# A two-layer hybrid decoder on eight cores: norm steps bound to engines, a later queueing rule in its planner, six residual tiles kept in SBUF, first loads in another order

## The reference

```
h = h + 1/2 * gate1 * SwiGLU_1(mod1(RMSNorm(h)))
h = h + gate2 * W_out[ SGU_heads(P) || DilatedAttn_heads(P) ],  P = mod2(RMSNorm(h)) @ W_in
h = h + 1/2 * gate3 * SwiGLU_2(mod3(RMSNorm(h)))
```

## Time and profile before

| | |
|---|---|
| three timed runs | 5645.67, 5723.91, 5064.55 us (median 5645.67) |
| profiled execution | 5035.81 us |
| its span, slowest core (2) | 5034.3 us; all cores 4988.7 to 5034.3 |
| PE / DVE / ACT / POOL busy | 95% / 54% / 39% / 23% of the span |
| DMA | 866.37 MB, mean 172 GB/s |

### The profile page before, as it was taken

How to read it: one execution, slowest core, us unless ns; L and a number is a source line. 1 busy time by engine, 2 the same in 40 slices (tenths; PEclk the granted TensorE clock), 3 DMA queues, 4 the chain that set the end, 5 groups by cost and what they waited for, 6 DMA issues and landing times.

```text
span 5034.3 us, 75361 instructions; the slowest of 8 cores (4988.7 to 5034.3 us)
## 1 busy us (share of the span) xinstructions
PE 4797.4 (95%) x25784; PEld 2274.2 (45%) x26282; DVE 2739.8 (54%) x4359; ACT 1957.7 (39%) x2862; POOL 1147.0 (23%) x955
## 2 busy tenths in 40 slices
PE   4999989989999999999999999999999999999998
PEld 1444434444445544444444444444444455544443
DVE  7542676483775464773433327755638654536424
ACT  4111556353554443411311126644536553524211
POOL 4001561131550101400200016402136200023101
PEclk9999999999999999999999999999999999999999
DMA  8968674687565686882621385757575545474237
GB/s 237 216 123 220 184 193 122 182 239 202 163 188 164 176 227 174 262 239 66 211 95 38 92 241 156 194 140 203 138 206 175 171 127 158 113 239 156 96 98 258
DMA packets 389049, 866.37 MB, mean 172 GB/s; under 512 B 151456, under 2 KB 184608, under 8 KB 382240
## 3 DMA queue, kind: packets, MB, share of 16 engines
q1 hardware_dynamic: 371344, 773.02, 49.6%
q0 software_dynamic: 17328, 88.49, 11.2%
HBM read 766.36 MB, written 241.17 MB: 200 GB/s over the span
## 4 chain that ended last, share of the span: by engine, by line
PE 77%; DMA 7%; DVE 5%; issue 4%; ACT 3%; POOL 2%; SPq 1%; DVEq 0%; POOLq 0%; ACTq 0%
PE ps L925 42%; PE ps L953 21%; PE ps L1052 6%; PE ps L1355 3%; PE ps L1293 3%; PE ps L1270 2%; DMA hS<-arena 2%; DMA arena<-hS 1%; DMA arena<-ada_w 1%; DVE arena L1112 1%; POOL arena L1121 1%; DVE arena L879 1%; DMA arena<-wdS 1%; DVE arena L860 1%; DMA vS<-arena 1%
## 5 line engine op out<-in xcount | busy, mean ns | idle before, releaser
L925 PE MATMUL ps<-arena 128*128 128x512 bf16 x10957 | 2486.5, 381 | 54.6 <-ACT arena L884 16.8
L925 PEld LDWEIGHTS ps<-arena 128*128 128x128 bf16 x11264 | 1077.4, 98 | 1308.4 <-issue 59.2
L953 PE MATMUL ps<-arena 128*128 128x512 bf16 x5501 | 1228.0, 380 | 19.8 <-DMA arena<-wdS 10.2
L931 ACT ACTIVATE arena<-ps 128x512 f32<-128x512 f32 x704 | 419.2, 597 | 1327.7 <-PE ps L925 1312.2
L953 PEld LDWEIGHTS ps<-arena 128*128 128x128 bf16 x5632 | 547.3, 98 | 673.2 <-issue 23.8
L933 DVE SCALAR_TENSOR_TENSOR arena<-arena,ps 128x512 f32<-128x512 f32 x704 | 480.4, 684 | 623.1 <-ACT arena L931 621.7
L957 DVE SCALAR_TENSOR_TENSOR arena<-ps,arena 128x512 f32<-128x512 f32 x256 | 192.0, 750 | 833.5 <-PE ps L953 794.0
L853 ACT ACTIVATE arena<-arena 128x512 f32<-128x512 f32 x448 | 270.0, 625 | 865.2 <-DMA arena<-hS 537.5
L1052 PE MATMUL ps<-arena 128*128 128x512 bf16 x2528 | 575.7, 386 | 21.8 <-DVE arena L1112 6.2
L938 DVE TENSOR_TENSOR arena<-ps,arena 128x512 bf16<-128x512 f32 x704 | 484.7, 690 | 185.0 <-PE ps L925 161.0
L860 POOL TENSOR_TENSOR arena<-arena 128x512 f32<-128x512 f32 (+1 forms) x236 | 316.0, 1339 | 1066.2 <-ACT arena L853 987.7
(11 more groups left out here) (71 smaller groups left out, 2600.2 us busy)
## 6 DMA issues: line engine op xcount, KB each, us to landing
arena<-wguS SPq DMA_DIRECT2D x242, 512.0 KB, 5.9
arena<-hS SPq DMA_DIRECT2D x192, 512.0 KB, 7.2
arena<-wdS SPq DMA_DIRECT2D x136, 704.0 KB, 7.2
arena<-ada_w SPq DMA_DIRECT2D x144, 512.0 KB, 6.2
hS<-arena SPq DMA_DIRECT2D x248, 256.0 KB, 5.8
arena<-hS SPq DMA_DIRECT2D x184, 256.0 KB, 6.0
wguS<-wgu POOLq DMA_DIRECT2D x66, 512.0 KB, 7.6
hS<-arena SPq DMA_DIRECT2D x64, 512.0 KB, 6.7
```

Source lines behind the costliest of these rows:

```text
L925: main([(lambda e, kc=kc, half=half, bk=bk, y=y, gu=gu: e.matmul(bank(bk), lhsT=gu[:, half, kc, :], rhs=y[:, kc, :], start=(kc == 0), stop ...
L931: G.op([act(lambda e, sg=sg, gb=gb: e.activation(out=smv[sg.i], in_=bank(gb), func=AF.Tanh, scale=0.5), 490, "tanh")], reads=[gb], writes= ...
L953: main([(lambda e, j=j: e.matmul(bank(bk), lhsT=wd[:, j, :], rhs=a[:, j, :], start=(j == 0), stop=(j == FC - 1)), [bwd, ba[j]], MM) for j ...
```

## The change

1. **The planner.** A side task that feeds others no longer gets a latest time of at most 30 us after its place; only what it feeds counts. A task that is no DMA, whose margined landing lies ahead and whose L is over 5 us past PE's next matmul, is not queued until the margined landing.
2. **Fixed engines.** sqsum and ropeadd, oamul, anorm go to POOL alone, nu to DVE alone, ny to ACT alone, vnorm to ACT or POOL. Only the norms of the first four tiles and of the last two keep a choice.
3. **Tiles summed in place.** `downs` takes tiles that are loaded whole at its start: tile 0, and tiles 4 and 6, of the first SwiGLU in both layers (whose next norm starts from SBUF and no longer loads them), and tiles 4 to 7 of the last SwiGLU, whose sums are not stored any more. Tile 7 was in place before, so six are new in that sense. Tiles 6 and 7 of the end share their down weights, tile 7 one chunk behind.
4. **First loads.** c and tile 0 of the input come first, then the rows of `ada_w`; the constants and the other tiles come later; the first weights get due times.

```
 priorities
-            L = t.cur + 30000.0
+            L = 1e12 if t.succ else t.cur + 30000.0
 schedule, pick
+                if not t.dma and t.mready > now and t.L > hp + 5000.0:
+                    nxt = min(nxt, t.mready)
+                    continue
 norm_sum(ht, pos, alts=False)
-                G.op([pool(f, 1250), dvex(f, 615)], reads=[ba, bq], writes=[bo], name="sqsum", pos=pos)
+                G.op([dvex(f, 615), pool(f, 1280)][:1 + alts] if alts else [pool(f, 1280)], reads=[ba, bq], writes=[bo], name="sqsum", pos=pos)
 norm_y
-                G.op([dvex(f, 615), pool(f, 1300)], reads=[brs], writes=[bh], name="nu", pos=pos)
+                G.op([dvex(f, 615), pool(f, 1700)][:1 + alts], reads=[brs], writes=[bh], name="nu", pos=pos)
-                      dvex(g, 420), pool(g, 1500)],
+                      dvex(g, 420)][:1 + alts],
 proj
-                            out=o, in_=i_, func=AF.Identity, scale=sc, bias=bi), 390), pool(f, 500), dvex(f, 200)],
+                            out=o, in_=i_, func=AF.Identity, scale=sc, bias=bi), 390), pool(f, 500)],
-                        G.op([pool(f, 1300), dvex(f, 650)], reads=[a0[1], a1[1]], writes=[bo], name="ropeadd")
+                        G.op([pool(f, 1400)], reads=[a0[1], a1[1]], writes=[bo], name="ropeadd")
-                    G.op([pool(f, 1300), dvex(f, 615)], reads=[bzt, ugs[hd][1]], accw=[boa], name="oamul", pos=pos)
+                    G.op([pool(f, 1300)], reads=[bzt, ugs[hd][1]], accw=[boa], name="oamul", pos=pos)
 normalise
-                        G.op([pool(f, 1300), dvex(f, 615)], reads=[ba, br], accw=[bo], name="anorm", pos=pos, part=h)
+                        G.op([pool(f, 1300)], reads=[ba, br], accw=[bo], name="anorm", pos=pos, part=h)
 FFN.downs
-            def downs(self, tiles, dst=None):
-                for m in range(KC):
-                    wd, bwd = load_wd(self.l, self.w, m, G.M)
-                    for t in tiles:
-                        self.down(t, m, wd, bwd, dst)
+            def downs(self, tiles, dst={}, keep=True, lag=0):
+                wd = {}
+                for t in dst:
+                    load_h(dst[t], t, self.src, self.bsrc, G.M)
+                for m in range(KC + lag):
+                    if m < KC:
+                        wd[m] = load_wd(self.l, self.w, m, G.M)
+                    for n, t in enumerate(tiles):
+                        k = m - lag * n
+                        if 0 <= k < KC:
+                            self.down(t, k, wd[k][0], wd[k][1], dst.get(t), keep)
 first loads
-            G.dma("sp", lambda e: e.dma_start(out=cb, in_=src), 524288, writes=[bcb], name="cb", pos=p0)
+            G.dma("sp", lambda e: e.dma_start(out=cb, in_=src), 524288, writes=[bcb], name="cb", pos=p0,
+                  due=None if due is None else due - 90000.0)
+                      due={1: -16000.0, 2: -13000.0, 3: -8000.0}.get(j))
-        cond(range(16), -3000.0, steps(WD0 + 4096, 4096, 3) + steps(ACT[0], 4096, 5), WD0, -26000.0)
+        cond(range(16), -3000.0, steps(WD0 + 4096, 4096, 3) + steps(ACT[0], 4096, 5), WD0, -28000.0)
 the stages
-            f1.downs((0, 1))
+            h0 = HT(HB)
+            f1.downs((0, 1), {0: h0})
+            norm_y(h0, 0, l, 1, pm)
+            nrm(1, 1, pm + 15000.0, H)
-            fa.downs((4, 5))
+            h4 = HT(HB)
+            fa.downs((4, 5), {4: h4})
-            fa.downs((6, 7))
+            h6 = HT(HB)
+            fa.downs((6, 7), {6: h6})
-                fc.downs((4, 5))
+                hts = {4: HT(HB), 5: HT(GU0)}
+                fc.downs((4, 5), hts, False)
-                fc.downs((6,))
-                fc.downs((7,), ht)
-                norm_out(norm_load(6, hS, bHS, G.M, GU0), 6, G.M - 25000.0)
-                norm_out(ht, 7, G.M, True)
+                hts = {6: HT(ACT[0]), 7: HT(ACT[1])}
+                fc.downs((6, 7), hts, False, 1)
+                norm_out(hts[6], 6, G.M, True)
+                norm_out(hts[7], 7, G.M, True)
```

More of the change, by code:

```diff
@@ L783, in load_gu @@
             if (l, w) == (0, 0) and (l, w, j) not in kept:
-                G.dma("pool", lambda e: e.dma_start(out=ap, in_=wgu_d[l, w, j]), 1048576, writes=[b], name="guf", pos=pos)
+                G.dma("pool", lambda e: e.dma_start(out=ap, in_=wgu_d[l, w, j]), 1048576, writes=[b], name="guf", pos=pos,
+                      due={1: -16000.0, 2: -13000.0, 3: -8000.0}.get(j))
                 G.dma("sp", lambda e: e.dma_start(out=wguS[l, w, j], in_=ap), 524288, reads=[b], writes=[bWG[l, w, j]],
@@ L869, in norm_sum, with norm_y @@
             return rs, brs
-        def norm_y(ht, slot, l, i, pos):
-            rs, brs = norm_sum(ht, pos)
+        def norm_y(ht, slot, l, i, pos, alts=False):
+            rs, brs = norm_sum(ht, pos, alts)
             y, by = tile(Y0 + 8192 * slot, [128, KC, T], BF16, KC, "y")
@@ L939, in gates, with down @@
                                   610)], reads=[ub, sg], writes=[ba[j]], name="hid", pos=p)
-            def down(self, t, m, wd, bwd, dst=None):
+            def down(self, t, m, wd, bwd, dst=None, keep=True):
                 a, ba = self.act[t]
@@ L1366, in outproj, with norm_load @@
             return ht
-        def norm_load(t, src, bsrc, pos, off=HB):
+        def norm_load(t, src, bsrc, pos, off=HB, due=None):
             ht = HT(off)
-            load_h(ht, t, src, bsrc, pos)
+            load_h(ht, t, src, bsrc, pos, due)
             return ht
         for ap, src, n in ((ng_sb, ngv, "ng"), (adab, ada_b, "adab"), (fg_sb, fgv, "fg"), (lngb, lngb_d, "lngb")):
-            G.dma("sp", lambda e, ap=ap, src=src: e.dma_start(out=ap, in_=src), 65536, writes=[bC[n]], name="const", pos=-20000.0, due=-90000.0)
+            G.dma("sp", lambda e, ap=ap, src=src: e.dma_start(out=ap, in_=src), 65536, writes=[bC[n]], name="const", pos=-20000.0, due=-21000.0)
         memset(ones_bf, 1.0, bC["ones"])
@@ L1388, in nrm @@
                 s, b = (src, bsrc) if src_ is None else src_
-                norm_y(norm_load(t, s, b, pos, off), t % 4, l, i, pos)
+                first = l == 0 and i == 0 and t == 0
+                norm_y(norm_load(t, s, b, pos, off, -60000.0 if first else None), t % 4, l, i, pos, l == 0 and i == 0 and t < 4)
             H = (hS, bHS)
@@ L1411, in build_nc @@
                 mx0.load(c, ACT[0] + 8192 * n, True, p2)
-            nrm(0, 1, pm, H)
-            nrm(1, 1, pm + 30000.0, H)
             mx0.open()
@@ L1434, in build_nc @@
             q3 = G.M
-            nrm(4, 1, q2, H)
+            norm_y(h4, 0, l, 1, q2)
             nrm(5, 1, q2 + 40000.0, H)
@@ L1451, in build_nc @@
                 if t == 4:
-                    nrm(6, 1, p4, H)
+                    norm_y(h6, 2, l, 1, p4)
                 if t == 5:
```

14 lines of the change are left out of this document (6 added, 8 removed).

## The result

Timed side by side, the changed kernel took 5546.82, 5004.09, 5733.06 and 5752.98 us (median 5639.94), the kernel before 5645.67, 5723.91, 5064.55 and 5073.81 us (median 5359.74). What is left gives a ratio of 0.9869 (0.9826 to 0.9911), 1.3% less. The profiled execution went from 5035.81 to 5004.09 us: 31.7 us less, where 59 less was forecast.

What follows compares the result with a forecast made beforehand. PE was taken to bound the kernel, busy 4797.4 of 5034.3 us, through its idle time and lower clock. Terms 30 + 12 + 8 + 9 + 0 = 59 us off 5035.81 gave 4977 us, range 4910 to 5040.

Steps and rivals of the forecast that it cites:

- more than that: Projections: many small PE waits also come from DVE's queue; 116 us less in all, 4920 us; chance 0.20.
- the waits move: Whole kernel: every removed wait is replaced, only the end and the tile in place gain; 5019 us; chance 0.17.
- VectorE's case: Projections: eight nu in a row on DVE delay rope if each takes over 1.76 us; 5107 us; chance 0.07.
- POOL's cases: Projections of tiles 0 to 3: POOL's added work outlasts PE's, cancelling the 30 us gain; 5041 us; chance 0.06.
- the 0.52 of clock to an idle microsecond: Four projection stretches: 40.6 us lost to lower clock over 78.6 us idle, so removed waits count 1.52 times.
- Fixed engines, 30 us: Projections: PE's waits for DVE's vnorm and last statistics go, 19.7 us, with clock 30; bounds nothing to 79.
- The later rule, 12 us: Side operations held until loads land: a good half of PE's 21.6 us exp and mask waits; bounds 0 to 27.
- Tiles in place, 8 us: Tile 0 goes to its next norm without store and loads: 5.3 us of ny waits, with clock 8; bounds 0, 8.
- The end, 9 us: Last tiles: down-weight waits 10.2 us and about 4 of clock go, later products cost 5.4; bounds 4 and 14.
- The start, 0: First gate 8.5 us earlier, but three norms follow it instead of two; bounds 9 us gained or lost.
- What should have shown it wrong: Projections: nu over 1.76 us with PE awaiting rope, POOL over 90%; new sqsum or nsum waits; first gate after 60 us.
- the signs of being right: No DVE vnorm or ropeadd waits, projection idle about 59 us, no late down-weight waits, earlier gate, shorter ACT square waits.

Runs made afterwards that it cites:

- e3: The kernel before with only the later queueing rule added: 5031 us, 5 less than the kernel before, ratio 0.9979.
- e10: The changed kernel without its queueing rule, on chip 0: 4978 us, 54 less than the kernel before, ratio 0.9902.
- e9: The whole changed kernel run again with more executions, on chip 0: 4945 us, 88 less than the kernel before, ratio 0.9831.
- e5: The whole changed kernel run again, unchanged, on chip 3: 4958 us on 3 of 8 dies, 80 less than the kernel before.

## Why the prediction was right or wrong

**The number.** The step that failed is that the sum starts from the profiled execution and takes the execution to be timed for one of that kind: a die that is held at a lower granted clock is put at nothing and lies outside the range, although two of the three timed runs on the table were 5645.67 and 5723.91 us. In three of the four executions timed, one die ran at a mean clock of 0.83 to 0.87, which makes the median 5639.94 us where 4977 was forecast. Executions of the profiled kind took 5001 to 5004 us at first, and 4945 and 4958 on dies at 0.98 or more later. Why a die is held at a lower clock in one execution and not in another, no run here shows.

**The size of the change.** 59 us were forecast, 32 measured at first, 80 to 88 without the 0.81. That lies between two of the cases, the forecast (4950 to 5005) and *more than that* (4920), so the forecast is too small, in the two terms named below; *the waits move*, VectorE's and POOL's cases are out.

**The reading behind it.** The 236.9 and 78.6 us of idle time came from a core with 498 matmuls unrecorded; the cores with all records had 175 to 200 and 45 to 64 in the same trace. The sum hardly suffered by it: its terms are priced by single waits, and of the rest it took only the 0.52 of clock to an idle microsecond, which is 37 / 76 = 0.48 in the mixer stages.

**Fixed engines, 30 us.** Right in size: 30 alone, 25 on top. It was made up a little otherwise: alone, the mixer stages lose 28 us of idle time and 24 of clock where 20 and 10 were counted, and some of that is given back elsewhere.

**The later rule, 12 us.** Mis-sized, and for the wrong wait. The term was a good half of PE's 21.6 us of waits for exp and mask. The rule alone leaves 17.0 us of them (e3), and without the rule the other parts leave only 3.3 (e10): it was their doing. ACT's 7.34 us before squares, on which most of the term rested, stayed and cost PE little. The wait of DVE for adarow, the smaller of the two in the rows, was the one that held PE, and it was read too small: 3.89 us in one place, 68.0 over the span of that core. The rule about halves it (44 to 20 us on top, 52 to 28 alone), which is worth 26 and 34 us on top but only 5 alone, where other waits took its place.

**Tiles in place, 8 us.** Mis-sized: the inner tiles give 35 alone, and 14 on top of the rest (25 less 11, if the end gives its 11 there too). I counted only PE's waits for ny and not what lies behind a norm that starts late, nor the clock with it; how that works is argued above and not shown. The tile is also not spared its store, as I had it.

**The end, 9 us.** Right: 11. There is no wait for down weights after 4930, and the two rows of eight products take 5.38 and 5.39 us.

**The start, 0.** Right in size: idle time goes from 67.2 to 60 us, 7 us, inside the bounds of 9 either way. The first gate is at 50.09, a little before the 52 to 56, and PE runs unbroken from 95.23 and not from 103.5: gate matmuls covered most of the third norm.

**What should have shown it wrong** did not: a nu takes 872 ns over the kernel, far under the 1.76 us of VectorE's case, and POOL is busy for 57% of the first projection, not 90. VectorE's case was priced too high besides: of eight nu at 2.09 us, 16.7 us, the banks cover 14.1, so 2.6 us a norm and not 6.6 would have reached PE. One of the signs of being right failed: ACT still waits up to 6.3 us before squares, where 4 or less was named. The Trainium skill's rule on GpSimd (GPSIMD Engine Reference, section Engine selection), about twice VectorE's time for two inputs, holds for the single sum: 1276 ns on POOL here against 689 on DVE. It decides nothing here: PE's waits for a POOL vnorm are 7.4 us, 1.8 the longest, and POOL's ropeadd even got shorter.

**What was not foreseen** is the 0.81: 30 to 99 us a core in the first trace, which took back much of what the shorter idle time had gained. It belongs to the execution and not to the kernel alone: it is absent from e9, on one die in e5, and in e3 on two cores of a kernel about as idle as the one before. What calls it up stays open, and so does whether the denser kernel meets it more often: 3 of 8 dies at 0.98 or more in e5 and 9 of 10 in e9 don't tell.

## What to carry to other kernels

In an in-order queue, look for the side operation that stands before its own transfer and ask what is queued behind it; its harm is that of the work behind it, here 11.65 us of TensorE for one late row of a side product. Price parts of a scheduling change both alone and taken out of the whole: 5 against 34 us for one and the same rule. Measure a stage between two marks in the program's work and not between two times: in stretches of fixed time the same kernel had 52 us idle in one trace and 70 in another, in the mixer stages 76 and 87. When idle time falls and the span does not, read the granted clock of stretches with no idle in them before looking for a new wait.
